# Experts' pass one of a decoder layer: another plan for the gathered rows, six choice steps of a dense tile moved into the query stage, first gates loaded piece by piece

## The reference, cut to what matters

```python
def peer_ffn(h, peer_wq, peer_subkeys, expert_u, expert_v):
    ...
    def block(xt):
        q = jnp.einsum('td,dc->tc', xt, peer_wq).reshape(PEER_BLOCK, PEER_HEADS, 2, D_KEY // 2)
        s = jnp.einsum('thcd,hckd->thck', q, peer_subkeys).astype(jnp.float32)
        sv, si = lax.top_k(s, PEER_TOPK)
        cand = (sv[:, :, 0, :, None] + sv[:, :, 1, None, :]).reshape(PEER_BLOCK, PEER_HEADS, PEER_TOPK * PEER_TOPK)
        cv, ci = lax.top_k(cand, PEER_TOPK)
        ...
        expert = i1 * N_KEYS + i2
        gate = jax.nn.softmax(cv, axis=-1)
        a = jax.nn.gelu(jnp.einsum('td,thkd->thk', xt, expert_u[expert]).astype(jnp.float32))
        return jnp.einsum('thk,thkd->td', (gate * a).astype(xt.dtype), expert_v[expert])
```

## Time and profile before

| what | value |
|---|---|
| median of 3 runs | 1975.55 us (1972.01 to 1976.75) |
| the profiled execution | 1967.81 us |
| its span, first to last instruction | 1966.0 us |
| query stage, projections of i = 0 to 15 | about 560 to 706 us |
| pass one, PE | 708.3 to 1406.9 us |
| seam, PE idle | 1406.9 to 1418.1 us |
| pass two, PE | 1418.1 to 1959 us |
| PE busy, DVE busy | 94%, 69% of the span |

### The profile page before, as it was taken

How to read it: one execution, slowest core, us unless ns; L and a number is a source line. 1 busy time by engine, 2 the same in 40 slices (tenths; PEclk the granted TensorE clock), 3 DMA queues, 4 the chain that set the end, 5 groups by cost and what they waited for, 6 DMA issues and landing times.

```text
span 1966.0 us, 29183 instructions
## 1 busy us (share of the span) xinstructions
PE 1843.4 (94%) x10246; PEld 1714.1 (87%) x10246; DVE 1360.7 (69%) x2739; ACT 708.7 (36%) x1362; POOL 426.3 (22%) x341
## 2 busy tenths in 40 slices
PE   5997799999999988989989989999799999999999
PEld 4875587678888888989979989999799899999999
DVE  2055233531125469999999999776489898999996
ACT  1012244421011033335646656665233333333333
POOL 0000000000000003333222232332234344444440
PEclk9898799977999998999999989999899999999999
DMA  8113421220222227977877879988889999999995
GB/s 279 46 62 93 118 76 53 79 61 12 88 63 65 65 91 264 319 253 263 314 270 283 289 248 343 337 307 326 295 303 380 367 375 387 395 384 393 386 394 178
DMA packets 190549, 457.28 MB, mean 233 GB/s; under 512 B 25843, under 2 KB 106227, under 8 KB 188403
## 3 DMA queue, kind: packets, MB, share of 16 engines
q1 hardware_dynamic: 142482, 258.11, 38.9%
q0 software_dynamic: 46192, 172.13, 23.8%
q10 hardware_dynamic: 1728, 25.17, 3.1%
HBM read 402.71 MB, written 56.05 MB: 233 GB/s over the span
## 4 chain that ended last, share of the span: by engine, by line
PE 41%; DVE 17%; issue 3%; DMA 2%; ACT 1%; SPq 0%; DVEq 0%; ACTq 0%
PE ps L1785 8%; PE ps L1788 8%; PE ps L1791 8%; PE ps L1761 6%; PE ps L1757 5%; PE ps L1758 5%; DVE sb_w_lo L1602 4%; PE ps L1807 2%; DMA sb_ring<-expert_v 2%; DVE sb_expert_row L1710 2%; DVE sb_one_hot L1703 2%; DVE sb_scores L1710 1%; DVE sb_hot L1629 1%; DVE sb_slot L1630 1%; DVE sb_hot L1625 1%
## 5 line engine op out<-in xcount | busy, mean ns | idle before, releaser
L1512 ACT ACTIVATE sb_w_hi<-sb_ring 128x1024 fp32r<-128x1024 f32 x256 | 271.2, 1060 | 525.3 <-PE ps L1791 251.7
L1602 DVE TENSOR_TENSOR sb_w_lo<-sb_ring,sb_w_hi 128x1024 fp32r<-128x1024 f32 x256 | 313.1, 1224 | 99.7 <-ACT sb_w_hi L1512 90.7
L1757 PE MATMUL ps<-sb_x_hi,sb_w_hi 128*128 128x384 f32 x1024 | 353.7, 345 | 2.1 <-ACT sb_w_hi L1512 2.1
L1758 PE MATMUL ps<-sb_x_lo,sb_w_hi 128*128 128x384 f32 x1024 | 348.9, 341 | 0.0
L1761 PE MATMUL ps<-sb_x_hi,sb_w_lo 128*128 128x384 f32 x1024 | 212.5, 351 | 46.0 <-DVE sb_w_lo L1602 45.9
L1761 PEld LDWEIGHTS ps<-sb_x_hi,sb_w_lo 128*128 128x128 f32 x1024 | 187.8, 195 | 53.5 <-DVE sb_w_lo L1602 53.4
L1785 PE MATMUL ps<-sb_x_lo,sb_w_hi 128*128 128x384 f32 x1016 | 199.8, 338 | 15.5 <-ACT sb_x_lo L1519 15.5
L1788 PE MATMUL ps<-sb_x_lo,sb_w_lo 128*128 128x384 f32 x1016 | 199.5, 338 | 0.0
L1791 PE MATMUL ps<-sb_x_lo,sb_w_hi 128*128 128x384 f32 x1016 | 198.1, 336 | 0.0
L1757 PEld LDWEIGHTS ps<-sb_x_hi,sb_w_hi 128*128 128x128 f32 x1024 | 195.1, 190 | 2.4 <-ACT sb_w_hi L1512 2.4
L1758 PEld LDWEIGHTS ps<-sb_x_lo,sb_w_hi 128*128 128x128 f32 x1024 | 194.9, 190 | 0.0
(11 more groups left out here) (308 smaller groups left out, 2653.1 us busy)
## 6 DMA issues: line engine op xcount, KB each, us to landing
sb_ring<-expert_u SPq DMA_DIRECT2D x128, 512.0 KB
sb_ring<-expert_v SPq DMA_DIRECT2D x128, 512.0 KB
gates_dense<-sb_g_stage ACTq DMA_DIRECT2D x12, 2048.0 KB
hid_dense<-sb_hid SPq DMA_DIRECT2D x112, 192.0 KB
sb_scores<-hid_dense SPq DMA_DIRECT2D x112, 192.0 KB
sb_g_stage<-gates_dense SPq DMA_DIRECT2D x32, 384.0 KB
sb_g_stage<-gates_dense SPq DMA_DIRECT2D x48, 256.0 KB
sb_region<-cache_cmp SPq DMA_DIRECT2D x64, 128.0 KB, 2.1
```

Of the source, the lines that this page charges most:

```text
L1512: nc.scalar.activation(whi[v % 2][:, :], ring(v)[:, :], ACT.Copy).then_inc(w_hi, 1)
L1602: nc.vector.tensor_tensor(wlo[v % 2][:, :], ring(v)[:, :], whi[v % 2][:, :], ALU.subtract).then_inc(w_lo, 1)
L1757: nc.tensor.matmul(out, hi[:, c * P:(c + 1) * P], g.x_hi[:, c], start=(c == 0), stop=False)
L1758: nc.tensor.matmul(out, hi[:, c * P:(c + 1) * P], g.x_lo[:, c], start=False, stop=False)
```

## The change

Three edits, all to the order of work; no arithmetic changes.

1. `EARLY = 6`: the first six choice steps of dense tile 0 (`best` for half-heads 0 to 11) are done in the query stage at i = 9 to 14, after that i's work for the row tokens, into buffers of their own (`sv_0`, `si_0`). The other 39 steps are spread over the same units of pass one: tile 0 now ends at unit 24 (33 before), tile 1 at 53 (59), tile 2 at 83 (85).
2. `ROW_PLAN`: the rows of pass one are taken at another pace. One a unit up to 35, then 40 rows in 51 units, then more than two a unit. Rows taken by the end of unit 35, 86, 115 and 127: 30, 70, 132, 160. Before: 40, 106, 144, 160. Pass two is the same.
3. SP issues the five pieces of the first gates one each at v = 124 to 128, not five in a row at v = 127.

```diff
+        S0 = g.S[:, 0].rearrange("p (i n) -> p i n", n=NKEY)
...
+                if KC < i <= KC + EARLY:
+                    h = i - KC - 1
+                    dve.wait_ge(s_act, 2 * h + 2)
+                    best(S0, (2 * h, 2 * h + 1), g.sv0, g.si0)
...
+ROW_PLAN = ((4, 0), (35, 30), (86, 70), (115, 132), (127, NR), (129, NR), (247, 2 * NR))
+EARLY = 6
 def dense_step_unit(d):
-    return 9 + d * 78 // 45
+    return 9 + (d - EARLY) * 76 // 39
...
 def rows_done(v):
-    if v < NKEY:
-        return max(0, v - 4) * NR // (NKEY - 5)
-    return NR + min(NR, max(0, v - NKEY - 1) * NR // 118)
+    for (v0, n0), (v1, n1) in zip(ROW_PLAN, ROW_PLAN[1:]):
+        if v <= v1:
+            return n0 + max(0, v - v0) * (n1 - n0) // (v1 - v0)
+    return 2 * NR
...
-                if v == NU - 1:
-                    for piece in range(len(PIECES)):
-                        load_gates(0, piece)
+                if NU - 4 <= v <= NU:
+                    load_gates(0, v - NU + 4)
```

More of the change, by code:

```diff
@@ L1326, in choices, with best @@
     crest = g.left[:, :].rearrange("p (n k) -> p n k", n=3)
-    sv, si, cand, cv, ci = g.sv, g.si, g.cand, g.cv, g.ci
-    def best(S, rows):
+    cand, cv, ci = g.cand, g.cv, g.ci
+    def best(S, rows, sv=g.sv, si=g.si):
         for k in rows:
@@ L1343, in best, with pairs @@
         link(last)
-    def pairs(heads):
+    def pairs(heads, sv=g.sv):
         v = sv[:, :, :].rearrange("p (h c) k -> p h c k", c=2)
@@ L1426, in experts @@
         block = ctx.enter_context(nc.Block())
-        dense_at = {dense_step_unit(d): d for d in range(FULL * STEPS)}
+        dense_at = {dense_step_unit(d): d for d in range(EARLY, FULL * STEPS)}
         group_at = {group_unit(n): n for n in range(NGRP)}
@@ L1607, in _, with places @@
             best, pairs, best_pairs = choices(nc, g, link)
-            def places(nh):
+            def places(nh, si=g.si):
                 n = nh * TOPK
@@ L1640, in dense_step @@
                 S = g.S[:, tile].rearrange("p (i n) -> p i n", n=NKEY)
+                sv, si = (g.sv0, g.si0) if tile == 0 else (g.sv, g.si)
                 if step < 8:
-                    best(S, (2 * step, 2 * step + 1))
+                    best(S, (2 * step, 2 * step + 1), sv, si)
                 elif step == 8:
-                    pairs(range(PH))
+                    pairs(range(PH), sv)
                     best_pairs((0,))
@@ L1651, in dense_step @@
                     best_pairs((6, 7))
-                    places(PH)
+                    places(PH, si)
                 elif step == 12:
@@ L1917, in build @@
         g.sv, g.si = sb("sv", [P, 2 * PH, TOPK]), sb("si", [P, 2 * PH, TOPK], U32)
+        g.sv0, g.si0 = sb("sv_0", [P, 2 * PH, TOPK]), sb("si_0", [P, 2 * PH, TOPK], U32)
         g.cand, g.left = sb("cand", [P, PH, NCAND]), sb("left", [P, 3 * NCAND])
```

## The result

The changed kernel took 1978.27 us (median; the kernel before 1971.22 in the same comparison): a ratio of **1.0042, 95% interval 1.0031 to 1.0054**, 8 us slower. 1972.5 us had been forecast, 3 us under the 1975.55 us that stood for the kernel before. The time lies in the range of 1951 to 1992 us, and the sign is on the other side. The profiled execution has a span of 1978.9 us.

The account below looks back on a forecast made before the run. DVE was taken to bound units 0 to 87, PE units 88 to 127 and pass two. -30 + 25 + 2 = -3 us, set against the median of 1975.55, gave 1972.5 us, range 1951 to 1992.

Parts of the forecast that it names:

- First stretch: Units 0 to 87, where DVE set the pace: 30 of 70 lost us won, bounds 25 to 38.
- The sum by a floor of PE and lumps of DVE on top: Units 0 to 87: PE needs 426.5 us without waits; bunched DVE work keeps 40 of the 70 lost us.
- Query stage: Six early choice steps of 2.84 us fit DVE's idle time before pass one: cost 0, no PE wait.
- Second stretch: Units 87 to 127: 90 rows gathered where 54 were; 25 us lost, bounds 0 to 51.
- the price of a gathered row: Units 87 to 127: a 10.1 us round over four buffers, 2.5 to 2.6 us for each row.
- rival C: Gathers in units 87 to 127 fall further behind, 2.75 us a row: +10 us, 1985.5 us; chance 0.25.
- Rival A: The forecast itself: rows cost 2.5 to 2.65 us in the mean, range -12 to +8 us; chance 0.50.
- The place in the second stretch: How the 25 us divide: 5 lost in units 87 to 114, 20 in units 115 to 127.
- The argument from bytes: Units 87 to 127 move 85.7 MB; at a limit of 390 GB/s that needs 220 us, against 206.
- rival B: The gathers keep up in units 87 to 127: -26 us, 1949.5 us; chance 0.20.
- The seam: Between unit 127 and pass two: a longer chain behind the last dot, 2 us lost.
- Rival D: Lumps, not the amount of work, held DVE; only 18 of 70 us return: +9 us, 1984.5 us; chance 0.05.

Follow-up runs that it names:

- e3: The changed kernel with more row buffers, eight for rows 70 to 131 and six from row 148 on; 31.7 us faster than the kernel before.
- e13: The changed kernel with the added row buffers and all five pieces of the first gates again at unit 127; about 10 us slower than e3.

## Why the prediction was wrong

- **First stretch: right.** -30 us were forecast at unit 88, and PE's unit 88 starts at 1173.96 instead of 1205.00: -31.0. DVE is busy 430 us (425 forecast). The stalls left are at units 5, 9 and at each tile's end. The sum by a floor of PE and lumps of DVE on top held for both edits together. It does not divide as it was told (17.0 and 41.4 us of DVE): edit 2 alone already gives 36, and edit 1 adds nothing to it.
- **Query stage: right**, no wait of PE, unit 0 within 1.1 us of its old start.
- **Second stretch: the mechanism right, the size wrong, and here the sign fell.** The step that failed is the price of a gathered row, 2.5 to 2.6 us; it was 2.8. 25 us were forecast as lost, 33.5 came (between PE's starts of units 88, 115 and 127, 144.7 + 52.8 us became 164.1 + 66.9). The term "8.1 us from issue to use, 1.15 for the dot, 0.8 until POOL issues again, 10.1 a round, 2.5 a row" measured 8.9, 1.2, 1.0 and 11.3, 2.8 a row (252.6 us for the 91 dots behind `w_lo` of unit 87). The 8.1 came from two waits of the kernel before, with two or three gathers in flight, and was taken for four. It is the median of the changed kernel's 86 gathers (8.12), but a queue is paid at the mean, and the mean is raised by the gathers beside the stores of gates, 11.4 us. 2.64 was the point from which rival C decides, and 2.8 is beyond it: **rival C came out**, priced at +10 us; +8 was measured. Its sum fits the trace: 252 - 209.6 = 42 us lost, and 33.5 + 7.2 at the seam = 40.7 came. Rival A's own range was not its sum: 2.65 us a row gives 238.5 - 209.6 = 29 us and +1, not the +8 that stood as its upper end.
- **The place in the second stretch: wrong.** 5 us were put on units 88 to 114, for four stores of gates that cut in, and these units lost 19.4; 20 were put on 115 to 127, and 115 to 126 lost 14.1. At 2.5 a row the first part would have been just kept up with; at 2.8, 59 rows need 165 us, and it took 164. The stores were named, and what they do to each gather beside them was not priced.
- **The argument from bytes: wrong.** It was to stand beside the round as a second witness for 2.6, with 380 to 400 GB/s as its sign. 341 and 357 GB/s were moved, and e3 moves 400 in the same units. The limit was not even the most of the trace before: 1258 to 1274 us there show 411 GB/s over 16 us, against the 394 that was read. Two limits that give the same number are not two proofs of it. "DMA: Bandwidth & Descriptors" of the Trainium skill, section "Measured", has 425 GB/s for a single large transfer; I set it beside rival B. The runs here come near it for short: e3 has two slices of 4.35 us at 430 GB/s and 417 over 50 us (1266 to 1316). A mean rate was not what decided.
- **The seam: the chain only half read.** +2 us were forecast and 7.2 came. The last dot came 8.1 us behind PE's last unit and not 3.5, which follows from the mis-sized rows, the ring load took 2.6 us longer, and the evacuation behind `w_hi` of unit 129 was not seen. "Edit 3 takes nothing from it" held for the gap; what it is worth with added buffers lies ahead of unit 127.
- **Rival D** (only 18 us come back up to unit 88) is out by the 31 that came, **rival B** by the waits.
- **Luck.** The time came within 6 us of the forecast because 31.0 us won and 40.7 lost nearly cancel; each size was worked out, and that their difference is small says nothing for either.

What stays open: what the 4 us between a gather's issue and its first bytes consist of, how the gain at the seam divides between its two orders, and what smaller or later stores of gates would give back.

## What to carry to other kernels

Before work that needs transfers is moved into a stretch where an engine has room, compare the pace asked for with what the buffers give, the mean round of a loaded transfer divided by the number of buffers, with the times in that mean when a large store runs beside it; where it exceeds that, move less (20 rows turned +8 us into -19) or add buffers first (-32). Price two cures of the same engine together, by the next engine's floor, and not one by one. At a seam, list for each engine in order what stands ahead of the instruction that the next stage waits for: a wait for the last of a set, and an evacuation queued behind a load, together cost 8.5 and 9.9 us in two kernels.

## What the runs showed of the hardware

- A gather of 128 rows of 4 KB had its last packet 7.1 us after its issue with four buffers in use, 8.8 in e3 with up to eight; its first packets came 4.2 and 6.1 us after the issue. Halving its bytes took only 1.4 us from issue to use.
- Beside a 2 MB store from ScalarE's queue the same gather needed 9.3 us to its last packet, and 6.2 without one (the changed kernel, 26 and 60 gathers).
- With gathers, ring loads and stores from three queues together the core moved 400 GB/s over 141 us and 417 over 50 (e3), more than the 386 of pass two.
- SyncE's own issue of a DMA took 3.0 us for the fifth of five pieces of gates in a row and 2.3 for the ring load behind it (e13), not 0.33 to 0.43. In the kernel before these were 2.75 and 0.86.
- PE's granted clock was 0.97 in stretches where it waited often (units 88 to 126 of the changed kernel) and 1.00 where it did not (the same units before, and e3), so that a wait costs more than its length: of the 33.5 us lost between PE's starts of units 88 and 127, 25.2 are its visible idle time.
